# Three pieces of a fixed order moved: a residual's value roundings, a scan's roots, a decay's running sums

## The chip, the cores and the metric

The kernel runs on one core of one Trainium2 chip. The metric is the time of one execution on the device in microseconds (us); the version before took 1071.31 us (median of three runs, 1070.12 to 1072.58).

## The reference

Three layers on a sequence of 256 tokens with 1024 features, all in float32. The first block is a mixer with three branches (sparse attention over selected keys, compressed/selected/windowed attention, and a state-space branch) and a feed-forward part; the second is a convolution and pooling mixer ("even"), then a recurrent mixer ("odd"), and a last norm. What the change touches:

```
# state-space branch: running sums of the decays
a_cum = jnp.cumsum(dtc * a, axis=2)
decay_states = jnp.exp(a_cum[:, :, -1:] - a_cum)

# residuals: after each part the sum is normed again and multiplied with the next weights
x = x + mix @ w_out[l];  h = rms_norm(x, norm2_g[l])
x = x + jnp.square(jax.nn.relu(h @ w_ff1[l])) @ w_ff2[l]
h = h + even_mixer(rmsnorm(h, norm_even[j]), ...)
h = h + odd_mixer(rmsnorm(h, norm_odd[j]), ...)

# odd mixer: gates, and a linear recurrence over time
r = sigmoid(xh @ w_rg + b_rg);  i = sigmoid(xh @ w_ig + b_ig)
log_a = -LRU_C * r * softplus(-lam);  a = exp(log_a)
mult = sqrt(-expm1(2.0 * log_a));  bterm = mult * (i * xc)
_, hs = lax.associative_scan(_lin_combine, (a, bterm), axis=1)
```

## The kernel before

**Products in three parts.** TensorE multiplies at full pace only in a rounded 32-bit format (fp32r). So each weight and each value is split: ScalarE writes the rounded part (`ring_hi` for weights, L1052; `arena_r` for values, L1080/L1082), and VectorE or GpSimd writes the remainder (`ring_lo`, L658; `arena_r`, L1363/L666). Each 128x128 block of weights then gives three matmuls: high by high, high by low, low by high (L2056 to L2058, or L1812 to L1814 where the tokens are the stationary side).

**The weights' way.** A stream of units of 512 KB (8 blocks of 128x128) goes by DMA into a ring of 5 places. `ring_hi` has only 3 places (`HIS = 3`), so the rounding of a unit must wait until the unit three before it has been multiplied. The rounding of a unit is put two units ahead (`AHEAD = 2`): the step `("wsplit", u + 2)` stands right before the step in which unit u starts. `on_gpsimd(u)` says which engine makes the remainder.

**The order.** `schedule()` writes one list of steps. Every engine's program walks through this list and issues, in the list's order, what is its own in each step. Nothing overtakes on an engine, so a step that waits holds what stands behind it on its engine, and on that alone. Semaphores join the engines. The step names used below:

- `("job", name, i)`: a projection, 24 matmuls with 8 blocks of weights; its result is read from one of three PSUM places.
- `("tm", name, half, u, t)`: one unit of a token-major product, for tokens t (two tiles of 128) and one half of the 1024 columns; `w_out` (residual 1), `ff2` (residual 2) and `even_ya` (residual 3) close with it. Two of these (t = 0, 1) make a unit, 12 matmuls.
- `("xt", q, half, t)`: four transposes of the new sum for residual q. `("split", tag, c)` and `("lo", tag, c)`: value rounding and its low part, from these transposes. `("xcopy", q, b)`: copies of them (q = 2, 3).
- `("acum",)`: running sums of the decays. TensorE multiplies with a triangle (L1831 to L1833); ScalarE copies `ac` and `run` (L931, L932), sends `run` to DRAM (L935) and takes an exponential (L937) of what VectorE has subtracted (L1432).
- `sA`, `sE`, `sR`, `sB`, `sC`: steps of the softmax (score L1904, its read by VectorE L1553, exponential L987, and so on); `("select", 1, quarter)`: a piece of the top-k choice on VectorE (L1499 to L1505); `pA`: the compression score (L1883).
- `("uroot", h)`: the square root for head h (L1110, 128x256). `("wcopy", m)`: a 512-wide copy (L1148) for the scan. `("rgi", h)`: the odd mixer's gate matmuls (L2013) and four activations (L1154 to L1160). `("oconv", j)`: VectorE's short convolution of the odd mixer (L1577 to L1583), which frees the PSUM place of job `xr` j. `("scan", h)`: L1713, L1714. `("gact", ...)`: gate activation, L1214 and L1725.

In `residual(q, tag)` the second half's first unit is followed by both transposes, the roundings of four value tiles with their low parts, and two copies; only then comes the second unit with the weight rounding that is put ahead of it. In the odd mixer's last `xr` job stand nine roots and the first copy. The running sums stand right behind the last step of the q norms, ahead of the first gate projection (`mg`).

The lines that the change moves among:

```
splits.setdefault(("units", u) if u < AHEAD else starts[u - AHEAD], []).append(("wsplit", u))
act.wait_ge(w_in[u % RING], 16 * (u // RING + 1))
act.wait_ge(filled["proj"], used[hi_before[u]])
```

Of the kernel before, what the change touches and what calls it, by code (L numbers as in the profile page):

```python
# [113 lines left out]
def schedule():  # L114

    out = []
    jobs = {name: [("job", name, i) for i in range(n)] for name, n, _ in PHASES}

    def token_parts(name):

        n = TOKENS[name]
        return [(u, t) for u in range(n) for t in range(NT)]

    def residual(q, tag=None):

        name, n = CLOSES[q], TOKENS[CLOSES[q]]
        for half in range(2):
            for u, t in token_parts(name):
                out.append(("tm", name, half, u, t))
                if half == 1 and u == 0 and tag:  # L130
                    out.append(("xt", q, 0, t))
                    if t == 1:
                        for c in range(4):
                            out.extend([("split", tag, c), ("lo", tag, c)])
                        if q > 1:
                            out.extend([("xcopy", q, 0), ("xcopy", q, 1)])
                if half == 1 and (u, t) == (n - 1, 1) and tag:
                    out.append(("xt", q, 1, 0))
                if u == n - 1:
                    out.extend([("res", name, half, t)])  # L140
                    if not tag:
                        out.append(("xg", half, t))
                    if tag is None or (half, t) != (1, 1):
                        out.append(("sq", q, half, t))
                    if not tag and half == 0:
                        out.append(("pre", t))
                    if not tag and half == 1:
                        out.append(("fin", t))
        if not tag:
            return  # L150
        out.append(("xt", q, 1, 1))
        for c in range(4, 8):
            out.extend([("split", tag, c), ("lo", tag, c)])
        out.append(("sq", q, 1, 1))
        if q > 1:
            out.extend([("xcopy", q, 2), ("xcopy", q, 3), ("stat", q)])
        else:
            out.append(("stat", q))
# [23 lines left out]
    for n, job in enumerate(jobs["dq"] + jobs["nq"]):  # L182
# [3 lines left out]
        if n % 2 == 1:  # L186
            out.append(("idx", n // 2))
        out += keys.get(n, [])
    out += [("qm", 15), ("qroot",), ("vcmp",), ("acum",)]

    soft = []
    for i in range(48 + 5):
        group = []

        for stage, lag in (("sB", 4), ("sC", 5), ("sA", 0), ("sE", 1), ("sR", 2)):
            if 0 <= i - lag < 48:
                group.append((stage, i - lag))
        group += {2: [("pA", 0)], 5: [("pB", 0)], 9: [("pT", 0), ("pA", 1)], 12: [("pB", 1)],
                  16: [("pT", 1)]}.get(i, [])
        if i in (0, 2, 4, 6):  # L200
            group.append(("select", 1, i // 2))
        soft.append(group)
    prep = [[("btr",)], [("xtr", 0)], [("xtr", 1)], [("st", 0)], [("xtr", 2)], [("st", 1)], [("xtr", 3)],
            [("st", 2)], [("xtr", 4)], [("st", 3)], [("xtr", 5)], [("xtr", 6)], [("xtr", 7)],
# [2 lines left out]
    for i in range(16 + 4):  # L207
        group = []
# [40 lines left out]
    for c in range(8):  # L249
        out += [("mgr", c), jobs["br_ssd"][c], ("split", "mix", c)]  # L250
    residual(1, "h1")
    for j in range(34):
        if j < 32:
# [3 lines left out]
        if j >= 2:  # L257
            out.append(("split", "ff", j - 2))
    residual(2, "h2u")
    out.append(("pads",))  # L260

# [52 lines left out]
    for c in range(8):  # L314
# [3 lines left out]
        if c % 2:  # L318
            out += even_yb[4 + c // 2] if c < 7 else []
    out += [("split", "ya", 7)] + even_yb[7]  # L320
    residual(3, "h3u")
    for j in range(12):
        out.append(jobs["xr"][j])
        if j == 1:
            out += [("bcast", 3), ("spread", 3)]
        if j > 0:
            out.append(("oconv", j - 1))
        if 2 <= j < 10:
            out += [("hf", 3, j - 2), ("split", "h3", j - 2)]
        if j == 11:  # L330
            out += [("uroot", h) for h in range(9)] + [("wcopy", 0)]
        elif j >= 2:
            out.append(("rgi", j - 2))
        if j >= 3:
            out.append(("lw", j - 3))
    gate = jobs["gate"]
    for j in range(12):
        out.append(gate[j])
        if j % 2 and j < 11:
            out.append(("wcopy", j // 2 + 1))  # L340
        if j < 3:
            out.append(("rgi", 9 + j))
        if j == 0:
            out.append(("oconv", 11))
        out.append(("scan", j))
        if j < 3:
            out.append(("lw", 9 + j))
        if j >= 2:
            out.append(("scanout", j - 2))
        out.append(("gact", gate[j]))  # L350
        if j == 5:
            out += [("uroot", h) for h in range(9, 12)]
        if j >= 3:
            out.append(("split", "ly", j - 3))
# [11 lines left out]
    out = final  # L366
# [47 lines left out]

def program(nc, x_t, x_tok, w_stream, w_tok, w_cmp, w_rgi, cols, rows, g_rows, out):
    steps = schedule()
    where, turns = psum_tenants(steps)
    slots = {"proj": 3, "score": 2, "turn": 1, "pv": 1, "mean": 1}
# [1729 lines left out]
```

How the kernel before makes its waits and increments, by code:

```python
        def readers_done(eng, key):  # L598
            g, n = where[key]
            prev = n - slots[g]
            if prev >= 0:
                for e in turns[g][prev]:
                    eng.wait_ge(read[g, e], sum(e in r for r in turns[g][:prev + 1]))
# [1 line left out]
        def was_read(eng, key, reader="A"):  # L606
            g, n = where[key]
            eng.wait_ge(read[g, reader], sum(reader in r for r in turns[g][:n + 1]))
# [45 lines left out]
        def remainder(eng, u):  # L655
            eng.wait_ge(sem("w_hi_ready"), hi_turn[u])
            return eng.tensor_tensor(ring_lo[:, u % RING, :, :].rearrange("p k n -> p (k n)"),
                                     ring[:, u % RING, :, :].rearrange("p k n -> p (k n)"),
                                     ring_hi[:, hi_slot[u], :, :].rearrange("p k n -> p (k n)").bitcast(F32),
                                     ALU.subtract)
# [1 line left out]
        def part_remainder(eng, tag, c):  # L663
            src, hi, lo, _, _ = parts[tag]
            eng.wait_ge(sem(f"hi_{tag}"), c + 1)
            return eng.tensor_tensor(lo(c), src(c), hi(c).bitcast(F32), ALU.subtract)
# [21 lines left out]
        @block.sync  # L688
# [8 lines left out]
                    sp_eng.dma_start(wcmp, w_cmp).then_inc(sem("wcmp_in"), 16)  # L697
                if u >= RING:
                    sp_eng.wait_ge(filled["proj"], used[u - RING])
                if u == first["job", "br_ssd", 4] // 8:
                    sp_eng.wait_ge(sem("pv_done"), 64)
                    sp_eng.dma_start(sbuf_s[:, :, :].rearrange("p a n -> p (a n)"), x_tok).then_inc(sem("xtok_in"), 16)
```

## Time and profile before

| what | value |
|---|---|
| median of three runs | 1071.31 us |
| the profiled execution, time / span | 1073.69 us / 1072.0 us |
| mean granted TensorE clock | 0.987 |
| TensorE busy | 1019.9 us, 95% |
| VectorE busy | 673.4 us, 63% |
| ScalarE busy | 618.6 us, 58% |
| GpSimd busy | 589.4 us, 55% |
| moved by DMA | 163.76 MB, mean 153 GB/s |

Times in a timeline are microseconds from the start of the span. PE is TensorE, DVE VectorE, ACT ScalarE, POOL GpSimd. A row's start and duration are those of one instruction or of several merged ones (x2 and so on); in brackets stands how long the engine was idle before it and what ended that. The granted clock is 1.00 for 2.4 GHz and 0.50 for 1.2 GHz. Records overlap by a little, since an engine starts the next instruction before the last one has drained.

### The profile page before, as it was taken

Reading aid. Unit: us, or ns where it says so; the run is one execution under the profiler, and the core shown is the slowest. Engines: PE = TensorE matmul, PEld = TensorE weight load, DVE = VectorE, ACT = ScalarE, POOL = GpSimd, SP = SyncE. Lnnn points to the kernel's source line nnn. Section 1 sums busy time; section 2 is a strip of 40 time slices with the busy share of each in tenths; the row PEclk is TensorE's granted clock in tenths of the full one; section 3 lists DMA queues with packets and bytes.
Section 4 is the critical chain, followed back from the end, with each engine's and each line's share of the span. In section 5 each row is a group of like instructions: output and inputs, shape, how many; then the busy total and the mean of one; then the engine's idle time right before and its main releaser. Section 6 shows DMA issues by size and latency. Waiting matters only on the chain. (4 is left out here: it accounts for less than half of the span.)

```text
span 1072.0 us, 19547 instructions
## 1 busy us (share of the span) xinstructions
PE 1019.9 (95%) x7235; PEld 922.5 (86%) x7235; DVE 673.4 (63%) x1441; ACT 618.6 (58%) x1246; POOL 589.4 (55%) x448
## 2 busy tenths in 40 slices
PE   8999999999999998889999999999899989899996
PEld 8799878888889997789989999878898977689985
DVE  7769687666564426685545554232699986478873
ACT  5455566766665448764446555344434548568853
POOL 3657344444545449844543434444768876467563
PEclk9999999999999998999999999999999999999998
DMA  8334333343333455435655555655555545634452
GB/s 311 99 119 138 119 118 99 101 120 116 100 102 116 153 177 169 153 97 178 216 180 174 180 185 187 197 176 177 158 158 158 182 152 157 216 119 146 140 171 95
DMA packets 45822, 163.76 MB, mean 153 GB/s; under 512 B 5216, under 2 KB 5280, under 8 KB 45216
## 3 DMA queue, kind: packets, MB, share of 16 engines
q1 hardware_dynamic: 43200, 158.25, 47.0%
q10 hardware_dynamic: 2528, 4.26, 1.4%
q8 instruction: 58, 0.95, 0.4%
q14 instruction: 36, 0.29, 0.1%
HBM read 161.41 MB, written 1.08 MB: 152 GB/s over the span
## 5 line engine op out<-in xcount | busy, mean ns | idle before, releaser
L658 POOL TENSOR_TENSOR ring_lo<-ring,ring_hi 128x1024 fp32r<-128x1024 f32 x176 | 425.1, 2419 | 280.3 <-ACT ring_hi L1052 279.5
L2056 PE MATMUL p_proj<-arena_r,ring_hi 128*128 128x256 f32 x1664 | 499.2, 300 | 11.0 <-POOL ring_lo L658 5.0
L2057 PE MATMUL p_proj<-arena_r,ring_hi 128*128 128x256 f32 x1664 | 473.9, 285 | 0.0
L2058 PE MATMUL p_proj<-arena_r,ring_lo 128*128 128x256 f32 x1664 | 473.8, 285 | 0.0
L1052 ACT ACTIVATE ring_hi<-ring 128x1024 fp32r<-128x1024 f32 x276 | 289.5, 1054 | 118.7 <-PE p_proj L1814 63.5
L2056 PEld LDWEIGHTS p_proj<-arena_r,ring_hi 128*128 128x128 f32 x1664 | 322.0, 194 | 27.8 <-issue 15.8
L2057 PEld LDWEIGHTS p_proj<-arena_r,ring_hi 128*128 128x128 f32 x1664 | 322.4, 194 | 7.2 <-issue 6.0
L2058 PEld LDWEIGHTS p_proj<-arena_r,ring_lo 128*128 128x128 f32 x1664 | 322.1, 194 | 0.0
L658 DVE TENSOR_TENSOR ring_lo<-ring,ring_hi 128x1024 fp32r<-128x1024 f32 x100 | 130.8, 1308 | 113.8 <-ACT ring_hi L1052 112.5
L1812 PE MATMUL p_proj<-ring_hi,arena_r 128*128 128x512 f32 x272 | 107.8, 396 | 8.0 <-POOL ring_lo L658 5.3
L1814 PE MATMUL p_proj<-ring_lo,arena_r 128*128 128x512 f32 x272 | 106.1, 390 | 0.0
L1813 PE MATMUL p_proj<-ring_hi,arena_r 128*128 128x512 f32 x272 | 106.0, 390 | 0.0
L773 POOL TENSOR_TENSOR sbuf_s<-sbuf_s,srow 128x256 f32<-128x256 f32 (+1 forms) x48 | 41.8, 871 | 83.3 <-DVE srow L1565 58.7
L1812 PEld LDWEIGHTS p_proj<-ring_hi,arena_r 128*128 128x128 f32 x272 | 51.1, 188 | 22.0 <-POOL ring_lo L658 7.8
L1082 ACT ACTIVATE arena_r<-arena 128x256 fp32r<-128x256 f32 x108 | 42.7, 409 | 39.5 <-DVE arena L1747 22.5
L1814 PEld LDWEIGHTS p_proj<-ring_lo,arena_r 128*128 128x128 f32 x272 | 51.1, 188 | 10.9
L1813 PEld LDWEIGHTS p_proj<-ring_hi,arena_r 128*128 128x128 f32 x272 | 51.1, 188 | 10.0
L666 POOL TENSOR_TENSOR arena_r<-arena,arena_r 128x256 fp32r<-128x256 f32 x59 | 45.5, 783 | 25.4 <-ACT arena_r L1082 25.4
L1214 ACT ACTIVATE th<-p_proj 128x256 f32<-128x256 f32 x44 | 16.9, 384 | 57.8 <-PE p_proj L2058 57.7
L1553 DVE CUSTOM_DVE_ANT_0 sbuf_s<-p_score,caus,nrq 128x128 f32<-128x128 f32 (+1 forms) x64 | 24.2, 415 | 41.0 <-PE p_score L1904 40.8
L1658 DVE SCALAR_TENSOR_TENSOR p_score<-arena,par,p_score 128x256 f32<-128x256 f32 x116 | 47.0, 483 | 1.2
L987 ACT ACTIVATE sbuf_s<-sbuf_s,srow 128x128 f32<-128x128 f32 (+1 forms) x96 | 42.6, 449 | 3.1 <-DVE srow L1553 3.1
(345 smaller groups left out, 1277.7 us busy)
## 6 DMA issues: line engine op xcount, KB each, us to landing
ring<-w_stream SPq DMA_DIRECT2D x286, 512.0 KB, 3.5
arena<-run_d ACTq DMA_DIRECT2D x11, 256.0 KB, 3.9
arena<-w_tok SPq DMA_DIRECT2D x1, 1632.0 KB, 12.6
arena<-w_rgi SPq DMA_DIRECT2D x1, 1536.0 KB, 6.1
wide_a<-run_d ACTq DMA_DIRECT2D x5, 256.0 KB, 4.0
arena<-x_t SPq DMA_DIRECT2D x4, 256.0 KB, 6.6
arena<-w_cmp SPq DMA_DIRECT2D x1, 1024.0 KB, 15.8
sbuf_s<-x_tok SPq DMA_DIRECT2D x1, 1024.0 KB, 5.6
```

The source lines that it names most:

```text
L658: return eng.tensor_tensor(ring_lo[:, u % RING, :, :].rearrange("p k n -> p (k n)"), ring[:, u % RING, :, :].rearrange("p k n -> p (k n)") ...
L666: return eng.tensor_tensor(lo(c), src(c), hi(c).bitcast(F32), ALU.subtract)
L987: ins = act.activation(p, p, ACT.Exp, bias=srow[:, i % 4, 2 + h:3 + h], scale=-1.0, accum_out=srow[:, i % 4, 4 + h:5 + h])
L1052: act.activation(ring_hi[:, hi_slot[u], :, :].rearrange("p k n -> p (k n)"), ring[:, u % RING, :, :].rearrange("p k n -> p (k n)"), ACT.Copy)\
L1082: ins = act.activation(hi(c), src(c), ACT.Copy)
L1658: ins = dve.scalar_tensor_tensor(out=A(AC + cc) if tap == CONV_K - 1 else acc, in0=ub[:, cc, tap:tap + S], scalar=col("even_cw", CONV_K * ...
L1812: pe.matmul(slot(key), hi, w_hi, start=(c == 0), stop=False)
L1813: pe.matmul(slot(key), lo, w_hi, start=False, stop=False)
L1814: mm = pe.matmul(slot(key), hi, w_lo, start=False, stop=(c == n - 1))
L2056: pe.matmul(slot(s)[:, 0:S], w_hi, hi, start=(c == 0), stop=False)
L2057: pe.matmul(slot(s)[:, 0:S], w_hi, lo, start=False, stop=False)
L2058: mm = pe.matmul(slot(s)[:, 0:S], w_lo, hi, start=False, stop=(c == n - 1))
```

## The change

Three places of the list are written otherwise; no instruction is added or left out.

```
                 if half == 1 and u == 0 and tag:
                     out.append(("xt", q, 0, t))
-                    if t == 1:
-                        for c in range(4):
-                            out.extend([("split", tag, c), ("lo", tag, c)])
-                        if q > 1:
-                            out.extend([("xcopy", q, 0), ("xcopy", q, 1)])
+                if half == 1 and (u, t) == (1, 0) and tag:
+                    for c in range(4):
+                        out.extend([("split", tag, c), ("lo", tag, c)])
+                    if q > 1:
+                        out.extend([("xcopy", q, 0), ("xcopy", q, 1)])
...
-    out += [("qm", 15), ("qroot",), ("vcmp",), ("acum",)]
+    out += [("qm", 15), ("qroot",), ("vcmp",)]
...
+        if i == 3:
+            group.append(("acum",))
...
         if j == 11:
-            out += [("uroot", h) for h in range(9)] + [("wcopy", 0)]
+            out += [("uroot", h) for h in range(4)]
...
         out.append(gate[j])
+        if j == 0:
+            out += [("uroot", h) for h in range(4, 9)] + [("wcopy", 0)]
```

Line numbers of the version after are 4 higher than those of before from the first softmax step on. The places where it matters:

ScalarE in the second half of residual 3, before. L1052 is a weight rounding, L1080 a value rounding, L898 a copy.

```order
L889 ACTIVATE sbuf_t,small<-sbuf_s 128x512
L1052 ACTIVATE ring_hi<-ring 128x1024
L1080 ACTIVATE arena_r_51<-p_turn,par 128x256
L1080 ACTIVATE arena_r_51<-p_pv,par 128x256
L1080 ACTIVATE arena_r_51<-p_turn,par 128x256
L1080 ACTIVATE arena_r_51<-p_pv,par 128x256
L898 ACTIVATE arena<-p_turn 128x2x256
L898 ACTIVATE arena<-p_pv 128x2x256
L1052 ACTIVATE ring_hi<-ring 128x1024 x3
```

The same place after:

```order
L893 ACTIVATE sbuf_t,small<-sbuf_s 128x512
L1056 ACTIVATE ring_hi<-ring 128x1024 x2
L1084 ACTIVATE arena_r_51<-p_turn,par 128x256
L1084 ACTIVATE arena_r_51<-p_pv,par 128x256
L1084 ACTIVATE arena_r_51<-p_turn,par 128x256
L1084 ACTIVATE arena_r_51<-p_pv,par 128x256
L902 ACTIVATE arena<-p_turn 128x2x256
L902 ACTIVATE arena<-p_pv 128x2x256
L1056 ACTIVATE ring_hi<-ring 128x1024 x2
```

One weight rounding, that of the half's fourth unit, has passed the value roundings. Residuals 1 and 2 change alike (residual 1 has no copies). TensorE's order in the residuals is the same as before.

ScalarE at the odd mixer's first gate, before (L1110 root, L1148 copy, L1154 and L1155 gate activations):

```order
L1052 ACTIVATE ring_hi<-ring 128x1024
L1110 ACT_TABLE_LOAD
L1110 ACTIVATE arena<-arena 128x256 x9
L1148 ACTIVATE p_turn<-arena 128x512
L1052 ACTIVATE ring_hi<-ring 128x1024
L1154 ACT_TABLE_LOAD
```

After:

```order
L1056 ACTIVATE ring_hi<-ring 128x1024
L1114 ACT_TABLE_LOAD
L1114 ACTIVATE arena<-arena 128x256 x4
L1056 ACTIVATE ring_hi<-ring 128x1024
L1114 ACTIVATE arena<-arena 128x256 x5
L1152 ACTIVATE p_turn<-arena 128x512
L1158 ACT_TABLE_LOAD
```

The weight rounding for the third gate job stands in the middle of the roots, with no further table load.

ScalarE at the running sums, before (L966 small copies, L1196 tanh of an mg job):

```order
L971 ACTIVATE root<-p_mean,small 128x64
L966 ACTIVATE vcl<-p_turn 15x64 x8
L931 ACTIVATE ac<-p_mean 128x96
L932 ACTIVATE run<-p_mean 64x128
L935 DMA run_d<-run 64x128
L937 ACT_TABLE_LOAD
L937 ACTIVATE dec<-dec 128x32
L1052 ACTIVATE ring_hi<-ring 128x1024
L1196 ACTIVATE arena<-p_proj 128x256
L1052 ACTIVATE ring_hi<-ring 128x1024
```

After:

```order
L975 ACTIVATE root<-p_mean,small 128x64
L970 ACTIVATE vcl<-p_turn 15x64 x8
L1056 ACTIVATE ring_hi<-ring 128x1024
L1200 ACT_TABLE_LOAD
L1200 ACTIVATE arena<-p_proj 128x256
L1056 ACTIVATE ring_hi<-ring 128x1024
L1200 ACTIVATE arena<-p_proj 128x256
L991 ACTIVATE sbuf_s,srow<-sbuf_s,srow 128x128 x2
L1056 ACTIVATE ring_hi<-ring 128x1024
```

The five rows of the sums are gone from here; they stand three jobs further down, without a table load of their own, ahead of the rounding for mg job 4. On TensorE the sums stand behind the fourth score pair, on VectorE the subtraction stands behind the second reciprocal of the softmax.

## Rows read from the trace of the kernel before

**Rows 1.** The page, part 1: busy time of each engine.

```profile
PE 1019.9 (95%) x7235; PEld 922.5 (86%) x7235; DVE 673.4 (63%) x1441; ACT 618.6 (58%) x1246; POOL 589.4 (55%) x448
```

**Rows 2.** Timeline of TensorE at the running sums: start, us, instruction [idle before].

```profile
115.49 0.24 PE L1865 MATMUL p_turn<-ident,kcr 64*64 64x64 f32 x1
117.53 0.43 PE L1831 MATMUL p_mean<-dta,upper 128*128 128x64 f32 x2 [1.80 <-ACT root L971]
...
118.46 0.38 PE L2056 MATMUL p_proj<-arena_r,ring_hi 128*128 128x256 f32 x1
...
122.92 0.59 PE L1904 MATMUL p_score<-kk_d,arena 128*128 128x256 f32 x2
...
126.22 0.60 PE L1904 MATMUL p_score<-kk_d,arena 128*128 128x256 f32 x2
```

**Rows 3.** Window there: busy us per engine, then granted clock, DMA share, GB/s.

```profile
120.00:122.00 2.00, 2.00 (x11) 2.00 (x10) 0.00 (x0) 1.84 (x3) 0.00 (x0) 0.50 0.06 16
```

**Rows 4.** Timeline of ScalarE at the running sums.

```profile
117.38 1.77 ACT L966 ACTIVATE vcl<-p_turn 15x64 f32<-15x64 f32 x8
...
120.15 1.28 ACT L937 ACT_TABLE_LOAD   x1 [0.56 <-ACT run L932]
...
121.58 1.04 ACT L1052 ACTIVATE ring_hi<-ring 128x1024 fp32r<-128x1024 f32 x1
...
123.40 1.05 ACT L1052 ACTIVATE ring_hi<-ring 128x1024 fp32r<-128x1024 f32 x1
```

**Rows 5.** Timeline of VectorE and GpSimd there, up to the second score's read.

```profile
122.72 1.23 DVE L658 TENSOR_TENSOR ring_lo<-ring,ring_hi 128x1024 fp32r<-128x1024 f32 x1 [2.84 <-ACT ring_hi L1052]
...
124.54 2.39 POOL L658 TENSOR_TENSOR ring_lo<-ring,ring_hi 128x1024 fp32r<-128x1024 f32 x1 [0.33 <-ACT ring_hi L1052]
...
124.64 2.57 DVE L1499 TENSOR_TENSOR arena<-arena,caus 128x256 f32<-128x256 f32 x1
127.25 0.43 DVE L1501 MAX8 m<-arena 128x8 f32<-128x256 f32 x1
...
129.22 0.35 DVE L1553 CUSTOM_DVE_ANT_0 sbuf_s<-p_score,arena,nrq 128x128 f32<-128x128 f32 x1
```

**Rows 6.** Timeline of residual 2: TensorE and ScalarE.

```profile
701.96 0.27 PE L1782 MATMUL p_turn<-ident,sbuf_s 128*128 128x128 f32 x1
...
705.86 2.00 ACT L1052 ACTIVATE ring_hi<-ring 128x1024 fp32r<-128x1024 f32 x2
...
709.42 0.50 PE L1812 MATMUL p_proj<-ring_hi,arena_r 128*128 128x512 f32 x1 [1.36 <-POOL ring_lo L658]
```

**Rows 7.** Timeline of residual 3, and a window of it.

```profile
928.02 0.27 PE L1782 MATMUL p_turn<-ident,sbuf_s 128*128 128x128 f32 x1
...
932.38 2.94 ACT L1052 ACTIVATE ring_hi<-ring 128x1024 fp32r<-128x1024 f32 x3
...
935.92 0.50 PE L1812 MATMUL p_proj<-ring_hi,arena_r 128*128 128x512 f32 x1 [1.81 <-POOL ring_lo L658]
...
934.00:936.00 2.00, 0.19 (x2) 0.08 (x1) 0.00 (x0) 1.32 (x2) 2.00 (x2) 1.00 0.57 139
```

**Rows 8.** Timeline of residual 1, TensorE.

```profile
558.24 0.50 PE L1812 MATMUL p_proj<-ring_hi,arena_r 128*128 128x512 f32 x1 [0.17 <-POOL ring_lo L658]
```

**Rows 9.** Timeline of the odd mixer's first gates.

```profile
987.96 2.87 ACT L1110 ACTIVATE arena<-arena 128x256 f32<-128x256 f32 x9
...
991.25 1.04 ACT L1052 ACTIVATE ring_hi<-ring 128x1024 fp32r<-128x1024 f32 x1
...
992.40 1.22 DVE L658 TENSOR_TENSOR ring_lo<-ring,ring_hi 128x1024 fp32r<-128x1024 f32 x1 [3.65 <-ACT ring_hi L1052]
...
996.28 0.38 PE L2056 MATMUL p_proj<-arena_r,ring_hi 128*128 128x256 f32 x1 [2.00 <-DVE arena L1583]
...
996.77 2.38 POOL L658 TENSOR_TENSOR ring_lo<-ring,ring_hi 128x1024 fp32r<-128x1024 f32 x1 [7.64 <-ACT ring_hi L1052]
...
1001.81 0.45 ACT L1154 ACTIVATE p_score<-p_score,half 128x256 f32<-128x256 f32 x1 [1.62 <-PE p_score L2013]
```

## The prediction

> **What bounds the kernel now.** I read the page's busy line first: TensorE is busy 95% of the span [rows 1]. So only two things can give time back: moments in which TensorE stands, and stretches in which it runs at the lower clock. The list of TensorE's waits says who ended those moments and where to look; then I read the timeline of each engine around the three edits.
>
> Running sums [rows 2]: TensorE's last small matmul starts at 115.49, then it waits 1.80 for the root, runs the sums from 117.53 to 118.46, and only then starts the first mg job. That job needs 4.46 us to its score pair at 122.92; the next job and score pair need 3.30 together (122.92 to 126.22). The granted clock is 0.50 there [rows 3], the lower of the two levels, 1.2 GHz, after the wait. ScalarE [rows 4] meanwhile copies the sums, issues a DMA, loads a table (1.28) and takes an exponential before it rounds the third job's weights at 121.58.
>
> Residuals: TensorE waits 1.36 [rows 6], 1.81 [rows 7] and 0.17 [rows 8] before the fourth unit of a second half, each time for GpSimd's remainder. The rounding ahead of it starts late because value roundings and copies stand before it on ScalarE.
>
> Gates [rows 9]: nine roots (2.87), a 512-wide copy, then the rounding at 991.25. VectorE stands 3.65 for it and does its remainder and then the last oconv; TensorE waits 2.00 for that. ScalarE itself later waits 1.62.
>
> **The change part by part.** Nothing is added or removed in work: the order on SP and GpSimd's queue is unchanged, ScalarE's DMA issue (run_d) moves with the sums, and the number of table loads stays.
>
> *Residuals.* ScalarE's rounding of unit 3 needs two things: the ring slot of unit 0, done when the second transpose group starts (701.96 and 928.02), and to be next in line. Now it is next. Residual 2: it starts at about 702.2 instead of 705.86; with 1.05 for itself and 2.4 for GpSimd the remainder is ready at 705.8, before TensorE asks at 708.06 (709.42 less 1.36). So 1.36 goes. Residual 3: the rounding of unit 2 before it ends at about 928.3, so 928.3 instead of 932.38, remainder at 932.0, TensorE asks at 934.11: 1.81 goes. Residual 1: 0.17 goes. What is late instead: the four value roundings, their low parts and the copies start about 0.6 to 1.1 later. Behind them on ScalarE stands the rounding of the next unit or job, and TensorE asks for that one a whole unit later (2.75 us, since the two units before the wait take 702.56 to 708.06). So I put this at zero. Sum 3.34; bounds 0 (slot or transfer late) and 3.34.
>
> *Gates.* The rounding stands behind four roots instead of nine and the copy. Nine take 2.87, so four end at 989.2 and it starts 2.05 earlier. VectorE's remainder starts at 990.35 instead of 992.40 and the last oconv ends 2.05 earlier, at 994.2, when TensorE's score pair is just over: the 2.00 wait goes, and with it, I expect, the low clock behind it. What is late next: ScalarE's total up to the first tanh is the same (five roots and the copy come after the rounding instead of before), so the gates' next remainder on GpSimd stays at 996.77 and is ready at 999.2; TensorE waits there about 1.0, the one after about 0.4. From then on ScalarE decides: it ran without a pause to 1000.2 and then waited 1.62 for the score pair of rgi 11, which TensorE now has done by 998.2. This 1.62 is what passes on to everything behind, since VectorE follows without a pause to the end of the gates. Term 1.6; bounds 0 and 2.0 (the wait itself).
>
> *Running sums.* TensorE starts the first mg job at 115.6 with full clock (the wait at 117.53 was ended by the root, so no weight was late there), and reaches its score pair at about 118.65 instead of 122.92: 4.27 earlier. The sums, now behind the fourth softmax step, cost 0.93 again (117.53 to 118.46). So 3.3, if nothing else binds. ScalarE: the third job's rounding comes right after the eight small copies, at 119.2, 2.4 earlier; the table load now follows it, and the fourth job's rounding starts at 121.8 instead of 123.40. VectorE's remainder for the third job ends at 121.55, TensorE asks at 122.2 (115.6 and twice 3.30); GpSimd's for the fourth ends at 125.3, TensorE asks after 127. The tight place is the compression score (L1883): it needs VectorE's read of the second score pair, and VectorE gets there only after the select step [rows 5]. Moved by 2.4 that read would end at 127.45, TensorE would stand 1.6 from 125.9, and only 2.4 less 0.93, 1.5, would be left; if the clock falls in that stall, it costs another 1.4 (4.46 against 3.30 less the 0.25 of the score pair) and the term is near 0. But the select step's first operation, L1499, took 2.57 only because it started 0.1 behind GpSimd's remainder and ended 0.3 after it (124.54 + 2.39 = 126.93 against 127.21); the 256-wide step after it takes 0.43. Now L1499 starts at 122.2, GpSimd's remainder at 122.9. L1499 escapes it, the select step ends 2 us sooner still, and TensorE does not stand. The new wait, ScalarE's exponential for VectorE's subtraction, holds the rounding for mg 4 until about 134.4; TensorE asks for it after 139, behind the fourth mg job, the sums and two xbc jobs. I take 3.2 (bounds 0 and 3.3), being nearest to the row of L1499.
>
> The Trainium skill, "GPSIMD Engine Reference", section Specifications, says that GpSimd shares its SBUF interfaces with VectorE and that they contend when a VectorE instruction has two SBUF inputs. The row of L1499 agrees. By this rule the residuals' low parts, which read PSUM and one SBUF tile, stay free beside the earlier remainders; without it, as if every VectorE operation waited, they would end 2 us later, still before the next unit is asked for.
>
> The Trainium skill, "ScalarE: Activation LUTs", section What ACT_TABLE_LOAD costs, gives a switch 1.28 for the load and 1.38 for a drain. The load at 120.15 ends at 121.43 and the rounding behind the exponential starts at 121.58 [rows 4], so no drain shows. By that page the third job's rounding would gain 3.8 and not 2.4, and the lower case of 1.5 would be 2.9; I keep the row.
>
> **Sum.** 3.34 + 1.6 + 3.2 = 8.1. The profiled execution took 1073.69 (span 1072.0); it would take 1065.6. The median of the three runs shown, 1071.31, lies 2.4 below the profiled one; from it: 1063.2.
>
> **Rivals.** *B, the select step still collides or TensorE stands at the compression score, perhaps with a low clock.* For it: the margin is 0.7 us and a 1.80 wait did bring 0.50. Against: the order of starts above. The running sums then give 0 to 1.5: 1064.9 to 1066.4, middle 1065.6. *C, the gates give nothing on*: GpSimd's unchanged 996.77 remainder sets the pace and VectorE loses the start. For: ScalarE's sum is unchanged. Against: the 1.62 pause. 1064.8. *D, the residual edit does not do what it says*: the rounding moves in the list but waits for its slot or its transfer. For: the gates' weights (w_rgi, 1.5 MB by its shape) load just before residual 3. Against: ScalarE's row 932.38 shows no wait of its own. 1066.5. *E, slower*: the clock. TensorE stands at several places without losing the clock, as for the 1.81 with 1.00 granted in 934 to 936 [rows 7]; the moments have moved, and each place at which the clock now falls costs 1.4 as at 118.46. With the gain of 8.1, six new falls are the point where it turns (1071.3 - 8.1 + 8.4 = 1071.6); eight give 1074.4, the time of this case. The same clock speaks for it (one 1.80 wait fell, one 1.81 did not); against it, that one fall in the first part and one at the gates go.
>
> **How the numbers follow.** Forecast 0.58, own range 1062.0 to 1064.8. B 0.17, C 0.12, D 0.08, E 0.05 (more than half of it fewer falls, 1066 to 1072). The runs of before spread by 1.2 to either side, so the range is 1061.2 to 1066.9. Bound of a measurable change: 0.2%, 2.1 us. Faster (below 1069.2) takes all but part of E: 0.94; same 0.04; slower 0.02.
>
> **What would show it.** Right: no wait before the first mg job and granted clock 1.00 around 116 to 122; L1499 near 0.5; no TensorE wait for GpSimd's remainder before unit 3 in residuals 2 and 3; the gates' wait for oconv gone, with about 1.0 before the next gate and no 1.62 pause on ScalarE. Wrong: a wait before L1883, a new wait on mg 4's remainder, a pause of ScalarE before the rounding of unit 3, or as many low-clock stretches as before.

## The result, and the profile after

The version after takes 1061.84 us (median of four runs, 1061.50 to 1063.34), the version before at the same time 1070.71; the ratio is 0.9912, interval [0.9899, 0.9925], so 9.4 us (8.0 to 10.8) were saved. The prediction said 1063.2 (1061.2 to 1066.9; 1062.0 to 1064.8 for its own case) and a gain of 8.1. The profiled execution of the version after took 1061.83 us, its span 1060.1, the mean granted clock 0.993.

The page's busy line of the version after; TensorE is busy 5.7 us less than in [rows 1] with the same instructions:

```profile
PE 1014.2 (96%) x7235; PEld 917.9 (87%) x7235; DVE 671.3 (63%) x1441; ACT 618.2 (58%) x1246; POOL 587.5 (55%) x448
```

**Running sums.** TensorE in the version after, start and duration; these rows answer to [rows 2]:

```profile
115.48 0.39 PE L2060 MATMUL p_proj<-arena_r,ring_hi 128*128 128x256 f32 x1
118.45 0.60 PE L1908 MATMUL p_score<-kk_d,arena 128*128 128x256 f32 x2
121.75 0.60 PE L1908 MATMUL p_score<-kk_d,arena 128*128 128x256 f32 x2
125.05 0.60 PE L1908 MATMUL p_score<-kk_d,arena 128*128 128x256 f32 x2
125.48 1.89 PE L1887 MATMUL p_score<-kk_c,arena 128*128 128x64 f32 x16
```

The first mg job starts right behind the last small product, without the wait of 1.80. The columns of the next view are busy time by engine, then the granted clock (the number before the DMA share):

```profile
115.00:120.00 5.00, 5.00 (x42) 4.86 (x41) 1.72 (x4) 4.79 (x12) 0.00 (x0) 1.00 0.36 110
120.00:125.00 5.00, 5.00 (x42) 4.95 (x42) 4.61 (x15) 4.64 (x10) 2.63 (x2) 1.00 0.56 194
```

So 1.00 stands where [rows 3] had 0.50, and a job with its score pair takes 3.30 and not 4.46. VectorE and GpSimd there, to compare with [rows 5]:

```profile
122.07 0.43 DVE L1503 TENSOR_TENSOR arena<-arena,caus 128x256 f32<-128x256 f32 x1
127.48 0.41 DVE L1525 TENSOR_TENSOR arena<-p_score,rq 128x240 f32<-128x240 f32 x1 [0.20 <-PE p_score L1887]
...
122.77 2.41 POOL L662 TENSOR_TENSOR ring_lo<-ring,ring_hi 128x1024 fp32r<-128x1024 f32 x1 [0.54 <-ACT ring_hi L1056]
```

L1503 (L1499 before) starts 0.70 ahead of GpSimd's remainder and takes 0.43 instead of 2.57. VectorE now waits for the compression score, not TensorE for VectorE. On ScalarE the table load at 120.06 is followed by the next activation at 121.36, and the rounding ahead of the load ends at 120.05, so the load costs its 1.28 and no more; that agrees with [rows 4] and speaks against the 1.38 for a drain in the Trainium skill, "ScalarE: Activation LUTs", section What ACT_TABLE_LOAD costs.

**Residual 3.** GpSimd's remainder for the fourth unit, and TensorE's first product of that unit, which had waited 1.81 in [rows 7]:

```profile
921.30 2.40 POOL L662 TENSOR_TENSOR ring_lo<-ring,ring_hi 128x1024 fp32r<-128x1024 f32 x1 [2.31 <-ACT ring_hi L1056]
...
925.84 0.39 PE L1816 MATMUL p_proj<-ring_hi,arena_r 128*128 128x512 f32 x1
```

The remainder is ready 2.1 before it is wanted. VectorE's four low parts of the values, which read PSUM, took 0.48 each beside it (921.70 to 923.86), as they did in residual 2 of before with GpSimd idle: the prediction expected them to stay free. The waits of [rows 6] and [rows 8] are gone as well.

**Gates.** TensorE, and ScalarE behind the roots (to compare with [rows 9]):

```profile
989.04 0.36 PE L2060 MATMUL p_proj<-arena_r,ring_hi 128*128 128x256 f32 x1 [1.02 <-ACT th L1218]
992.58 0.36 PE L2060 MATMUL p_proj<-arena_r,ring_hi 128*128 128x256 f32 x1 [0.43 <-POOL ring_lo L662]
...
989.84 0.45 ACT L1158 ACTIVATE p_score<-p_score,half 128x256 f32<-128x256 f32 x1
```

The waits of 1.0 and 0.4 are there as forecast, though the first is put down to ScalarE's tanh, which ended at 989.01, and not to GpSimd's remainder, which had ended 0.13 earlier (986.53 and 2.35). ScalarE starts the last gate's activations at 989.84 without the pause of 1.62.

**Where the 11.9 us between the two profiled executions went.** I took stretches between places at which TensorE waits in both versions. Such a difference is good to some 0.03 us: seven other kernels run below that share the version after's first stretch had 33.82 to 33.84 in it.

| stretch | before | after | gained |
|---|---|---|---|
| root's table load to the score pair behind the choice (115.87 to 153.11) | 37.24 | 33.83 | 3.41 |
| state step, end of the wait of 5.26 to end of that of 1.32 (409.88 to 476.53) | 66.65 | 65.29 | 1.36 |
| 483.30 to the transposes after residual 1 (562.11) | 78.81 | 77.31 | 1.50 |
| to those after residual 2 (746.04) | 183.93 | 182.22 | 1.71 |
| residual 3 (914.37 to 939.80) | 25.43 | 23.33 | 2.10 |
| gates (960.79 to 1019.98) | 59.19 | 57.56 | 1.63 |
| start, and all between | | | 0.15 |

The second row, and 1.00 of the third, lie where the change moves nothing. What they are is taken up below.

### The profile page after: what moved, and what is told of

The parts are those of the page before. It is cut to its first block and busy times, and to the rows that moved or that the text cites. A ratio compares the mean times of both kernels' runs of the same rounds, so it can differ in the third digit from the quotient of the medians.

```text
span 1060.1 us, 19547 instructions
## 1 busy us (share of the span) xinstructions
PE 1014.2 (96%) x7235; PEld 917.9 (87%) x7235; DVE 671.3 (63%) x1441; ACT 618.2 (58%) x1246; POOL 587.5 (55%) x448
```

## The experiments

"The stretch" of a part is the row of that table. Each kernel was profiled once; the ratio is to the version before.

**One part at a time.** e1 has only the first hunk of the diff, e2 only the two on the roots, e3 only the two on `acum`.

> The version before with the residual part alone. Theory (each part is worth what TensorE's own wait was, and nothing is given back): 3.3 to 3.8 us faster than before; the waits of 1.36 and 1.81 before the fourth unit of residuals 2 and 3 are gone, those at the running sums (1.80) and at the gates (2.00) stay. The pair of traces puts residual 2 at 1.71 and residual 3 at 2.1, above the 1.36 and 1.81 of the waits: if that surplus is real, it shows here again. Rival (the parts help one another, for instance the residual gains only because the clock stayed up): below 2 us. TensorE's stall near 483 us should still be followed by a low granted clock (0.70 in 485 to 490), if the fall there hangs on what ran before it and not on chance, since nothing ahead of it is changed.

> The version before with the roots in two batches alone. Theory: 1.6 us faster than before, the length of ScalarE's pause of 1.62 and not of TensorE's wait of 2.00; TensorE waits about 1.0 and 0.4 before the next two gates. Rival (the gates pass nothing on): 0 to 0.4. Rival (the whole wait and the low clock behind it come back): 2.0 to 2.6.

> The version before with the running sums moved alone. Theory: 3.2 to 3.6 us faster than before, all of it at 115 to 126 us, with granted clock 1.00 there. The rest of the 4.9 that the pair of traces shows by 442 us is a chance difference of the clock at 405 to 450 us. Rival (the shift by 3.6 us also changes how the clock falls at 405 to 450 and at 483 us, and does so each time): 5 to 6.4 us faster, with 1.00 granted in 485 to 490. If the sum of this run's gain and the two others' is within 0.5 of the whole change's 9, the parts are independent.

| kernel | median us | ratio | own stretches |
|---|---|---|---|
| e1, residuals | 1068.11 | 0.9967 [0.9955, 0.9980] | residual 2 182.23, residual 3 23.33 |
| e2, gates | 1070.70 | 0.9993 [0.9983, 1.0002] | gates 57.58 |
| e3, sums | 1068.68 | 0.9970 [0.9959, 0.9982] | sums 33.83 |

Times of before in that comparison: 1072.08 (1069.42 to 1074.68, 33 runs). The three gains are 3.5, 0.8 and 3.2 us, 7.5 in all with about 2.1 to either side, against 9.4. That is further off than the 0.5 that I had asked for, but within the noise. The medians thus can't say whether the parts add up; the stretches can. Each part's stretch is as short alone as in the version after, and those that a kernel doesn't touch keep the length of before (residual 2 183.92 in e2 and 183.91 in e3; gates 59.23 in e1 and 59.20 in e3). The parts are independent. Residual 1 shows in e3 against after, both at full clock from 483 on: 77.81 and 77.31, so 0.50. Residual 3, which e2 and e3 leave alone, took 25.27 and 25.28 in them with a wait of 1.65, against 25.43 with 1.81 in before: its gain is 1.9 to 2.1.

The surplus that e1 asked about is real: 1.36, 1.81 and 0.17 of wait returned 1.71, 2.10 and 0.50. TensorE of the version before at residual 2's wait ([rows 6] has the row at 709.42 with the wait):

```profile
707.44 0.39 PE L1813 MATMUL p_proj<-ring_hi,arena_r 128*128 128x512 f32 x1
707.67 0.39 PE L1814 MATMUL p_proj<-ring_lo,arena_r 128*128 128x512 f32 x1
...
709.76 0.40 PE L1813 MATMUL p_proj<-ring_hi,arena_r 128*128 128x512 f32 x1
```

The pace is 0.23 (707.44 to 707.67). From 707.67 to 709.42 are 1.75, so 1.52 were lost before the row; the wait in brackets, 1.36, leaves out the overlap of one matmul with the next (0.39 less 0.23). The next product starts 0.34 behind it and not 0.23. Together 1.63 to 1.7.

**The room that the sums depend on.**

```
+                        for _ in range(5 if t == 1 else 0):
+                            link(dve.max(m8[:, :], acc))
                         link(dve.tensor_tensor(acc, acc, caus[:, t, 0:kl], ALU.add))
```

> The version after, with five more 256-wide maximum searches (0.43 each, about 2.3 us with their gaps) on VectorE ahead of the first piece of the second token tile's top-k choice: it stands in for the 2.14 us that L1499 took longer before (2.57 against 0.43). Theory: this room is what the running sums' gain hangs on; the read of the second score pair ends at about 127.5 and not 125.2, TensorE asks for its place at 125.48 and stands 2.0 us before the compression score (L1887), so 2.0 slower than after (7.0 to 7.4 faster than before), and up to 1.4 more if the granted clock falls behind that stall (5.6 to 6.0 faster). Rival (VectorE's late reads don't reach TensorE, other room hides them): no stall and 9 to 9.4 faster than before.

1069.06 us, ratio 0.9969 [0.9957, 0.9981]. TensorE, VectorE and GpSimd in e4, and the windows behind:

```profile
127.61 2.00 PE L1889 MATMUL p_score<-kk_c,arena 128*128 128x64 f32 x16 [2.51 <-DVE srow L1559]
...
123.86 1.07 DVE L1505 TENSOR_TENSOR arena<-arena,caus 128x256 f32<-128x256 f32 x1
...
122.24 2.40 POOL L662 TENSOR_TENSOR ring_lo<-ring,ring_hi 128x1024 fp32r<-128x1024 f32 x1 [0.54 <-ACT ring_hi L1056]
...
125.00:130.00 5.00, 2.49 (x20) 2.39 (x20) 3.98 (x17) 0.97 (x5) 3.48 (x4) 0.96 0.32 105
130.00:135.00 5.00, 5.00 (x31) 4.85 (x29) 4.69 (x14) 2.29 (x6) 0.40 (x1) 0.70 0.00 0
```

The stall came where expected, at 127.6, and the clock fell to 0.70 behind it. It was 2.51 long and not 2.0: the first piece of the choice (L1505 here) now started beside GpSimd's remainder and took 1.07 instead of 0.43, so VectorE was held up by 2.9 and not by the 2.1 that the padding stands for. The sums' stretch, from the root's table load on, took 38.10 (33.83 in the version after). That is rival B's mechanism, real; with somewhat more delay than before had, it costs 4.27, more than the sums' gain of 3.41. The whole lost more than I expected (some 6 us by the ratios and not 2.0 to 3.4), since the stretches from 410 (66.70) and 483 (79.05) were the long ones here as well.

**L1503 beside GpSimd.** The first piece of the choice stands behind the second softmax step:

```
-        if i in (0, 2, 4, 6):
+        if i in (1, 2, 4, 6):
             group.append(("select", 1, i // 2))
```

> The version after, with the first piece of the second token tile's top-k choice behind the read of the second score pair instead of ahead of it. VectorE would come to its first operation (L1503, two SBUF inputs, 0.43 in after) at about 123.3, while GpSimd's remainder (122.77 to 125.18) runs. Theory (such an operation waits until GpSimd's has ended): it takes about 2.2 and ends at 125.3 or later, the read of the third pair moves to about 127.3, and TensorE, which has the second read early, stands for less than 0.5 at the compression score. Rival (its 2.57 in the version before had another cause, as its place in the order): 0.43 again. Whole kernel within 0.7 of after by either.

VectorE, and GpSimd's remainder beside it:

```profile
122.97 2.30 DVE L1503 TENSOR_TENSOR arena<-arena,caus 128x256 f32<-128x256 f32 x1
...
122.58 2.41 POOL L662 TENSOR_TENSOR ring_lo<-ring,ring_hi 128x1024 fp32r<-128x1024 f32 x1 [0.54 <-ACT ring_hi L1056]
```

2.30, with its end 0.28 after GpSimd's: the same instruction took 0.43 in the version after, so the length comes from the order of the two starts. By the rule in the Trainium skill, "GPSIMD Engine Reference", section Specifications, the two contend. The rows agree and say more: L1503's end follows the other's end (0.28 behind it here, 0.28 in before, 0.29 in e4), whatever its own start was. TensorE stood nowhere at the compression score, but VectorE's work ran 1.1 late and TensorE stood 1.60 at 144.78, with 0.67 granted in 145 to 150. The profile names no releaser there; in e8 as in the version after TensorE starts 0.1 behind the end of VectorE's short convolution (L1587, which ends at 144.67 and 143.62). Ratio 0.9935 [0.9920, 0.9949]: 1.7 slower than after by the spans (1061.8 and 1060.1) and 2.5 by the ratios, where I allowed 0.7.

**How many roots ahead of the rounding.** The diff of e5 against after; e6, e11 and e12 have 0, 8 and 9:

```
-            out += [("uroot", h) for h in range(4)]
+            out += [("uroot", h) for h in range(7)]
...
-            out += [("uroot", h) for h in range(4, 9)] + [("wcopy", 0)]
+            out += [("uroot", h) for h in range(7, 9)] + [("wcopy", 0)]
```

> The version after, with seven roots ahead of the weight rounding instead of four (two behind it). Between two of TensorE's waits that all versions have (950.58 and 1008.14 us in the version after) lie 57.56 us; with nine roots and the copy ahead 59.19. Theory (the start of that rounding sets it, and the loss grows with what stands ahead): three roots are 0.96 later than after, against 2.05 for five roots and the copy; TensorE waits about 0.9 for the last short convolution, ScalarE pauses 0.5 to 0.6 later, and the stretch takes 58.1 to 58.2. Rival (a step: either the low clock behind the wait or nothing): 57.6 or 59.2. Whole kernel: 0.6 slower than after, about 8.8 faster than before.

> The version after, with no root ahead of the weight rounding and all nine behind it: the rounding may start up to 1.28 earlier still. Theory (once TensorE no longer waits for the short convolution, ScalarE's total of roots, copy and gate activations sets the pace): the same stretch takes 57.4 to 57.7, as in the version after, and TensorE's waits of 1.02 and 0.43 stay or grow. Rival (the rounding's start still decides): 56.3. Rival (roots later delay the scan): over 58.

> The version after, with eight roots ahead of the weight rounding. The same stretch of the gates took 57.56 with four, 57.56 with seven (TensorE waited 0.85) and 59.19 with nine and the copy (2.00). Theory (only the clock's fall turns the wait into loss): TensorE waits about 1.15; 57.6 if 1.00 is granted behind it, about 58.4 if the clock falls. Rival (a loss that grows with the wait, from some point on): 57.9 with the clock at 1.00.

> The version after, with nine roots ahead of the weight rounding and only the copy behind it. Theory (only the clock's fall turns the wait into loss): TensorE waits about 1.5; 57.6 to 57.7 if 1.00 is granted behind it, about 58.7 if the clock falls. Rival (a loss that grows with the wait, from some point on): 58.2 with the clock at 1.00.

e5: 1062.51, ratio 0.9920 [0.9905, 0.9935]; e6: 1062.03, the same ratio; e11 and e12 one time each, 1064.29 and 1063.85 (both had a fall of the clock behind 479 us, far ahead of the gates). The gates' stretch:

| ahead of the rounding | TensorE's wait for oconv | clock behind it | stretch |
|---|---|---|---|
| 0 roots (e6) | none | 1.00 | 57.58 |
| 4 (after) | none | 1.00 | 57.56 |
| 7 (e5) | 0.85 | 1.00 | 57.56 |
| 8 (e11) | 1.16 | 1.00 | 57.57 |
| 9 (e12) | 1.46 | 1.00 | 57.59 |
| 9 and copy (before) | 2.00 | 0.66 | 59.19 |

The theory of e5 fell: nothing grows with what stands ahead. Up to 1.46 the wait costs nothing, and at 2.00 it costs 1.6. TensorE of e12 at its wait of 1.46, and the window behind:

```profile
987.53 0.39 PE L2060 MATMUL p_proj<-arena_r,ring_hi 128*128 128x256 f32 x1 [1.46 <-DVE arena L1587]
...
990.00:995.00 5.00, 4.86 (x38) 4.57 (x37) 4.66 (x11) 4.97 (x11) 3.31 (x2) 1.00 0.34 105
```

The fall is no matter of one trace: e1 and e3, which leave the gates alone, have it as before has, with 0.50 granted in 992 to 994 and stretches of 59.23 and 59.20. TensorE of before takes 4.47 from the gate job behind the wait (996.28) to the last gate's score pair (1000.75), e5 2.98 (984.35 to 987.33). That 1.49 is nearly all of ScalarE's pause of 1.62. That speaks for the clock; the next run tests it.

**The same wait with the clock kept up.** Version before, eight products that nobody reads ahead of the waiting job (the trace records each as two, so x16 below, 1.95 us):

```
+        if j == 2:
+            out.append(("pebusy", 8))
         out.append(gate[j])
...
+                    for _ in range(s[1]):
+                        pe.matmul(bank["mean"][0][:, 0:P], ones[:, :], mean_d[:, :], start=True, stop=True)
```

> The version before, with eight extra 128x128 matmuls on TensorE (some 0.22 each at 2.4 GHz, 1.8 in all, their result is never read) ahead of the gate job that waits 2.00 us for the last short convolution. The wait for the convolution stays as long as it was, but TensorE works in it. Theory (what the gates lost was not the wait but the lower clock behind it: with 1.00 granted TensorE reaches the last gate's score pair in time for ScalarE, whose pause of 1.62 shrinks to about 0.1): the stretch that takes 59.19 in before and 57.56 in after takes 57.6 to 57.8, the granted clock behind the place is 1.00, the whole is 1.5 faster than before. Rival (the wait itself is what was lost): 59.2, the same as before.

```profile
995.10 1.95 PE L1768 MATMUL p_mean<-mean_d,ones 128*128 128x128 f32 x16
...
995.00:1000.00 5.00, 4.79 (x41) 4.57 (x40) 4.65 (x11) 4.93 (x12) 2.25 (x1) 1.00 0.32 105
```

The clock stayed at 1.00 (0.66 in the window of before) and the stretch is 57.89, 1.30 of the 1.63 back with the roots and the wait for the convolution where they were. So at least 1.3 of the gates' 1.63 was the clock; the other 0.3 is not accounted for. The median does not show it: 1070.95, ratio 0.9996 [0.9982, 1.0010]. In the profiled execution the lower clock at 115 to 125 (0.66 and 0.66 against 0.93 and 0.73) took 1.2 of it back.

**Filling the two longest waits of the version after** the same way, with 22 and 11 products:

> The version after, with extra 128x128 matmuls whose result is never read in TensorE's two longest waits: 22 (4.8 us) in the one of 5.26 at 401 to 406 us and 11 (2.4 us) in the one of 2.73 at 437. Theory (it is idleness that lets the clock fall): 1.00 granted from 400 to 450, and 2.5 to 2.9 faster than after, from 5.54 against 3.65 us between the first products behind the long wait and 5.99 against 5.0 behind the other; that is a ratio to before of 0.9885 to 0.989. Rival (the clock falls at its own times, or the extra matmuls delay the work): no gain, or slower.

1061.83 us, ratio 0.9912 [0.9890, 0.9933], the same as the version after. The windows of e10, and of after below them:

```profile
400.00:405.00 5.00, 5.00 (x48) 4.83 (x48) 3.62 (x4) 4.88 (x15) 5.00 (x6) 1.00 0.71 234
405.00:410.00 5.00, 3.86 (x32) 3.12 (x31) 3.90 (x9) 4.94 (x13) 5.00 (x6) 1.00 0.26 83
```

```profile
400.00:405.00 5.00, 1.04 (x12) 0.67 (x11) 3.14 (x2) 4.88 (x15) 5.00 (x5) 0.88 0.76 256
405.00:410.00 5.00, 3.70 (x20) 3.37 (x21) 3.53 (x11) 4.94 (x15) 5.00 (x6) 0.50 0.35 102
```

The clock did as the theory said, 1.00 and a mean of 0.998, and no time came back: TensorE stands 0.96 at 409.05 for VectorE instead, and the stretch is 65.30 (65.29). ScalarE and GpSimd are busy 4.9 and 5.0 of 5 there in both. The low clock cost nothing here, since TensorE was not the late one.

That takes away my reading of the 1.36 in the table as a clock fall. VectorE and GpSimd of the version before, in the same stretch:

```profile
435.21 2.25 DVE L666 TENSOR_TENSOR arena_r<-arena,arena_r 128x256 fp32r<-128x256 f32 x1
...
434.77 2.40 POOL L658 TENSOR_TENSOR ring_lo<-ring,ring_hi 128x1024 fp32r<-128x1024 f32 x1
```

and of the version after:

```profile
430.70 0.88 DVE L670 TENSOR_TENSOR arena_r<-arena,arena_r 128x256 fp32r<-128x256 f32 x1
...
431.24 2.60 POOL L662 TENSOR_TENSOR ring_lo<-ring,ring_hi 128x1024 fp32r<-128x1024 f32 x1
```

It looks like L1499's collision again. In all 14 profiled executions that low part lasts 0.43 to 1.12 if it starts ahead of the remainder, and then the stretch is 65.23 to 65.59; it lasts 2.25 to 2.68 if it starts behind, and the stretch is 66.65 to 66.85. In the closest pair it started 0.05 ahead (e1, 0.43) and 0.01 behind (e3, 2.68); the longer ones of the first kind, as the 0.88 above, end 0.28 behind a shorter operation of GpSimd (430.00 to 431.30). No run moved this pair on purpose, so the cause rests on the 14 agreeing. Both sides occur with the sums moved (six short, four long) and unmoved (two and two), so I don't count the 1.36 to the change; with so few executions it is not shown that both sides are as likely with it as without.

**Values two units down.**

```
-                if half == 1 and (u, t) == (1, 0) and tag:
+                if half == 1 and (u, t) == (2, 0) and tag:
```

> The version after, with the value roundings, low parts and copies of a residual's second half one unit further down (behind the weight rounding of one more unit). Theory (what was put at zero in the forecast is zero with room to spare): residual 2's stretch, from the first transposes behind residual 1 (555.66 in after) to those behind residual 2 (737.88), stays at 182.2, and residual 3's (906.25 to 929.58) at 23.3, each within 0.3. In residual 2 the rounding behind the values would start about 2 us after its place in the ring is free, less than the 3.66 that cost 1.36 before. Rival (the values are needed early, or the next weights are late): 1 to 2 us given back in at least one residual, with a new TensorE wait for GpSimd's or VectorE's remainder or for the values.

1063.21 us, ratio 0.9929 [0.9912, 0.9945]. Residual 3 kept its 23.34, but in residual 2 a wait is back, one unit later:

```profile
707.97 0.50 PE L1816 MATMUL p_proj<-ring_hi,arena_r 128*128 128x512 f32 x1 [0.62 <-POOL ring_lo L662]
```

It costs 0.97 from 478 us on (260.50 against 259.53): 0.62 and the 0.35 that every such wait cost. I had missed that VectorE's remainder of that unit now stands ahead of the low parts, for which ScalarE waits 1.21. One unit down is free, two are not.

## Why the prediction was right

*Residuals* (3.34 forecast, 4.31 measured). The mechanism held at all three places and nothing was given back; "I put this at zero" was right, with less than a unit's room (e7). The term was mis-sized, and its upper bound of 3.34 was no bound: it took the bracketed wait for the loss, and each wait costs about 0.33 more (0.35, 0.29, 0.33). Rival D is out by e1.

*Gates* (1.6 forecast, 1.63 measured). The size was right, as was reading it off ScalarE's pause and not off TensorE's wait. The sentence "ScalarE decides" holds. What the forecast treated as a side effect ("and with it, I expect, the low clock") was most of the cause: the wait by itself was free at 1.46 (e12), and at 2.00 with the clock kept up the stretch lost 0.3 (e9). The new waits of 1.0 and 0.4 were right in size; the first one's releaser was another. Rival C is out by e2's stretch; its median alone would not have excluded it.

*Running sums* (3.2 forecast, 3.41 measured). L1503 was expected to start at 122.2 and GpSimd's remainder at 122.9, and started at 122.07 and 122.77. Rival B was the right danger: with the room more than filled (e4) the whole of the gain goes. The term holds the clock's fall too: all four kernels that keep the wait of 1.80 have it. In e2 and e9 it lasted longer than in before (0.70 and 0.62 in 115 to 120 and 120 to 125; 0.66 and 0.66; before 0.93 and 0.73), and their stretch took 38.70 and 38.41, so in some executions this part is worth up to 4.9.

*Sum.* 4.31 + 1.63 + 3.41 = 9.35, against 9.4 (8.0 to 10.8) by the ratio. The time, 1061.84, lies 1.4 under the forecast and 0.2 under the narrower range of its own case: 0.6 of that is the version before, which took 1070.71 this time and not 1071.31, and the rest goes with the 1.0 that the residuals' term lacked. That the wider range held it owes something to its width, which the prediction doesn't work out from the spread of 1.2. The profiled pair's other 2.5 is the collision (1.36), the clock behind the wait at 483 (1.00) and the start. That fall at 483 came after a wait of 1.64 to 1.66 in six of the 14 executions and not in the other eight, with the sums moved and unmoved; what decides it stays open. It may hang together with the collision: the fall followed five of the six long state steps (e3 is the sixth) and one of the eight short ones (e1). Rival E asked for six new falls, and none was seen that the change brought.

## What to carry to other kernels

Move what nobody waits for behind what TensorE will want, and check two things: what stands ahead of it now, and which operations with two SBUF inputs on VectorE will start just behind a long one on GpSimd. In this kernel a wait of TensorE was worth its bracket plus about a third of a microsecond where TensorE was the late engine, and nothing where it was not; a fall of the clock behind it added 1.0 to 1.75 at 483, 1.4 in e4 and 1.3 at the gates. With effects under 3 us, compare stretches between fixed waits and not medians: this kernel's spread by 2.5 to either side.

## What the runs showed of the hardware that I had not expected

Products whose result nobody reads, put into a wait, kept 1.00 granted (5.18 us of them in a wait of 5.26). An operation of 0.4 us on VectorE that started 0.01 behind GpSimd's took 2.68, and 0.05 ahead of it 0.43. And the same wait of TensorE (1.65) is followed by a fall of the clock in one execution and not in another.
